# Modulation products over one k tile of 1024 columns instead of two of 512, with eight portions moved to earlier stages

## The reference

```python
c_act = jax.nn.silu(c)
cc_act = jax.nn.silu(c_ctx)
mod_x = jnp.split((c_act @ w_mod + b_mod)[:, None, :], 6, axis=-1)
mod_c = jnp.split(cc_act @ w_mod + b_mod, 6, axis=-1)
hx = modulate(rms_norm(x, g_pre_mix), mod_x[0], mod_x[1])
hc = modulate(rms_norm(xc, g_pre_mix), mod_c[0], mod_c[1])
...
y_x = jnp.concatenate([a_x, gla_out(gla_x, gx, out_g)], axis=-1) @ w_out
x = x + mod_x[2] * rms_norm(y_x, g_post_mix)
f_x = swiglu(modulate(rms_norm(x, g_pre_ffn), mod_x[3], mod_x[4]), w_ffn_in, w_ffn_out)
x = x + mod_x[5] * rms_norm(f_x, g_post_ffn)
```

## Time and profile before

| | before |
|---|---|
| median of 3 runs | 2784.82 us (2784.71 to 2785.11) |
| the profiled execution, span from first to last instruction | 2783.2 us |
| around the span (median less span) | 1.6 us |
| TensorE busy | 2765.4 us (99%) |
| VectorE busy | 2253.5 us (81%), 3613 instructions |
| ScalarE / GpSimd busy | 377.3 / 368.5 us |
| moved by DMA | 571.81 MB, 205 GB/s |

### The profile page before, as it was taken

How to read it: one execution, slowest core, us unless ns; L and a number is a source line. 1 busy time by engine, 2 the same in 40 slices (tenths; PEclk the granted TensorE clock), 3 DMA queues, 4 the chain that set the end, 5 groups by cost and what they waited for, 6 DMA issues and landing times.

```text
span 2783.2 us, 35947 instructions
## 1 busy us (share of the span) xinstructions
PE 2765.4 (99%) x13588; PEld 2424.0 (87%) x13588; DVE 2253.5 (81%) x3613; ACT 377.3 (14%) x713; POOL 368.5 (13%) x462
## 2 busy tenths in 40 slices
PE   9999999999999999999999999999999999999998
PEld 8888888888888888888888888888888888888887
DVE  7988888999999999998886568978888888766554
ACT  3221112001111111110002121211200000000000
POOL 1111221011112121120111002201011111000000
PEclk9999999999999999999999999999999999999999
DMA  8787666677676666667786455557566776566553
GB/s 273 239 254 226 209 205 204 216 244 227 212 210 209 210 212 212 206 227 270 263 265 178 144 159 144 158 160 227 175 216 213 220 220 204 173 174 190 174 174 121
DMA packets 276381, 571.81 MB, mean 205 GB/s; under 512 B 25370, under 2 KB 26778, under 8 KB 275696
## 3 DMA queue, kind: packets, MB, share of 16 engines
q1 hardware_dynamic: 244528, 460.18, 53.6%
q0 software_dynamic: 31248, 109.01, 12.4%
q10 hardware_dynamic: 432, 0.34, 0.0%
HBM read 565.49 MB, written 3.93 MB: 205 GB/s over the span
## 4 chain that ended last, share of the span: by engine, by line
PE 81%; issue 15%; DVE 1%; DMA 1%; POOLq 0%; POOL 0%; DVEq 0%; SPq 0%; ACT 0%
PE PS L565 76%; PE PS L646 1%; PE PS L608 1%; PE PS L740 0%; PE PS L709 0%; PE PS L575 0%; DMA ring<-in_w_in 0%; DVE x_tok L1719 0%; DMA x_tok<-in_x 0%; PE PS L1004 0%; PE PS L905 0%; PE PS L987 0%; PE PS L625 0%; PE PS L828 0%; POOL mem L2323 0%
## 5 line engine op out<-in xcount | busy, mean ns | idle before, releaser
L565 PE MATMUL PS<-sums,mem 128*128 128x256 f32 x4056 | 1206.3, 379 | 0.0
L565 PE MATMUL PS<-ring,mem 128*128 128x256 f32 x3788 | 1071.0, 379 | 0.0
L565 PEld LDWEIGHTS PS<-sums,mem 128*128 128x128 f32 x4056 | 770.6, 190 | 104.8
L565 PE MATMUL PS<-ring,act_t 128*128 128x256 f32 x3076 | 832.8, 379 | 0.1
L565 PEld LDWEIGHTS PS<-ring,mem 128*128 128x128 f32 x3788 | 715.5, 190 | 97.7 <-issue 1.6
L565 PEld LDWEIGHTS PS<-ring,act_t 128*128 128x128 f32 x3076 | 578.6, 190 | 77.5 <-issue 1.6
L1093 DVE TENSOR_TENSOR sums<-ring 128x512 f32<-128x512 f32 x431 | 312.2, 724 | 272.6 <-PE PS L565 242.4
L1214 DVE SCALAR_TENSOR_TENSOR mem<-mem,small 128x512 f32<-128x512 f32 x480 | 358.5, 768 | 36.3 <-DMA mem<-in_w_mod 5.6
L1103 DVE TENSOR_TENSOR sums<-sums,ring 128x512 f32<-128x512 f32 x431 | 306.6, 711 | 33.6 <-issue 1.3
L1105 DVE TENSOR_TENSOR sums<-sums,ring 128x512 f32<-128x512 f32 x431 | 303.0, 703 | 33.1 <-issue 1.3
L565 PE MATMUL PS<-sums,act_t 128*128 128x256 f32 x1092 | 324.8, 379 | 0.0
(11 more groups left out here) (277 smaller groups left out, 1266.2 us busy)
## 6 DMA issues: line engine op xcount, KB each, us to landing
ring<-in_w_in SPq DMA_DIRECT2D x240, 512.0 KB, 3.8
mem<-in_w_mod POOLq DMA_DIRECT2D x192, 512.0 KB, 5.0
ring<-in_w_up SPq DMA_DIRECT2D x176, 512.0 KB, 3.9
ring<-in_w_ffn_in SPq DMA_DIRECT2D x176, 512.0 KB, 3.7
ring<-in_w_down SPq DMA_DIRECT2D x88, 512.0 KB, 4.4
ring<-in_w_ffn_out SPq DMA_DIRECT2D x88, 512.0 KB, 3.8
ring<-in_w_out SPq DMA_DIRECT2D x64, 512.0 KB, 4.1
ring<-in_w_branch_a SPq DMA_DIRECT2D x16, 512.0 KB, 3.7
```

Source lines behind the costliest of these rows:

```text
L565: mm = pe.matmul(product(g, j), of(j, 2 * (c if part is None else part) + q), weights(j, n, q), start=lead and j in OPENS, stop=tail, skip ...
```

## The change

One load is now one k tile x 1024 columns (4 KB for each partition, 512 KB as before), and a portion is one product over 1024 columns for each vector, not two over 512. A block has 1024 columns and 16 portions. `acc` has one buffer of 1024 columns for each vector. The reduce at a block's end goes over 1024 columns. The number of portions stays 192. `HALVES` gives every unit of the gate stage three portions (the even ones had two), and the branch projections twelve instead of eight; the eight of the second output projection are gone. GpSimd's counts follow.

```diff
-MOD_BLOCKS = ([(b, False) for b in (16, 17, 18, 19, 14, 15, 8, 9)] + [(b, True) for b in range(8)]
-              + [(b, False) for b in (10, 11, 12, 13, 20, 21, 22, 23)])
+MOD_BLOCKS = ([(b, False) for b in (8, 9, 7, 4)] + [(b, True) for b in range(4)]
+              + [(b, False) for b in (5, 6, 10, 11)])
...
-    for _j in range(1, 4 if _k % 2 else 3):
+    for _j in range(1, 4):
         HALVES[N0["gate"] + 4 * _k + _j] = 1
-for _k in range(1, 16, 2):
-    HALVES[N0["branch"] + _k] = 1
+for _k in range(16):
+    if _k % 4 != 2:
+        HALVES[N0["branch"] + _k] = 1
...
-for _k in range(4, 12):
-    HALVES[N0["wout2"] + _k] = 1
...
-        wm = cut(26880, 2, 2, CN)
-        acc = cut(28928, 2, CN)
+        wm = cut(26880, 2, 2 * CN)
+        acc = [cut(28928, 2 * CN), cut(25856, 2 * CN)]
...
-                    b, part = h // 8, h % 8
+                    b, part = h // 16, h % 16
                     blk, two = MOD_BLOCKS[b]
-                    vectors = ((0, 0), (1, 16)) if two else ((b % 2, 16),)
+                    vectors = ((0, 0), (1, 16)) if two else ((0, 16),)
                     ve.drain()
                     ve.wait_ge(wm_loaded[h % 2], 16 * (h // 2 + 1))
-                    for k in range(2):
-                        if k:
-                            ve.drain()
-                        for which, at_ in vectors:
-                            col = c_vec[:, at_ + 2 * part + k:at_ + 2 * part + k + 1]
-                            if part + k == 0:
-                                op = ve.tensor_scalar(acc[:, which, :], wm[:, h % 2, k, :], col, None, MUL)
-                            else:
-                                op = ve.scalar_tensor_tensor(acc[:, which, :], wm[:, h % 2, k, :], col,
-                                                             acc[:, which, :], MUL, ADD)
+                    for which, at_ in vectors:
+                        col = c_vec[:, at_ + part:at_ + part + 1]
+                        if part == 0:
+                            op = ve.tensor_scalar(acc[which], wm[:, h % 2, :], col, None, MUL)
+                        else:
+                            op = ve.scalar_tensor_tensor(acc[which], wm[:, h % 2, :], col, acc[which], MUL, ADD)
                     op.then_inc(s["wm_used"], 1)
-                    if part == 7:
+                    if part == 15:
...
-                    kt, col = 2 * (h % 8), CN * MOD_BLOCKS[h // 8][0]
-                    pool.dma_start(wm[:, h % 2], w_mod[:, kt:kt + 2, col:col + CN]).then_inc(wm_loaded[h % 2], 16)
+                    kt, col = h % 16, 2 * CN * MOD_BLOCKS[h // 16][0]
+                    pool.dma_start(wm[:, h % 2], w_mod[:, kt, col:col + 2 * CN]).then_inc(wm_loaded[h % 2], 16)
...
-                mod_loads(2 + u % 2)
+                mod_loads(3)
...
-            mod_loads(22)
+            mod_loads(26)
...
-            mod_loads(7)
             post_rstd(0)
             ffn2_rstd()
-            mod_loads(1)
```

More of the change, by code:

```diff
@@ L87 @@
         HALVES[N0["up2"] + 8 * _k + _j] = 1
-assert sum(HALVES.values()) == 8 * len(MOD_BLOCKS)
-SUMS = [(0, 8, 16, N0["down"] + 25), (8, 20, 18, N0["down"] + 35), (20, 28, 20, N0["wout2"] + 13),
-        (28, 32, 24, N0["up2"] + 66)]
+assert sum(HALVES.values()) == 16 * len(MOD_BLOCKS)
+SUMS = [(0, 8, 8, N0["down"] + 25), (8, 20, 9, N0["down"] + 35), (20, 28, 10, N0["wout2"] + 13),
+        (28, 32, 12, N0["up2"] + 66)]
 SUMS_AFTER = {_n: _b for _b, (_, _, _, _n) in enumerate(SUMS)}
 for _, _, _blocks, _n in SUMS:
-    assert sum(HALVES.get(_k, 0) for _k in range(_n - 1)) >= 8 * _blocks
+    assert sum(HALVES.get(_k, 0) for _k in range(_n - 1)) >= 16 * _blocks
 BANK7, THROUGH7 = [], []
@@ L1200, in mod_halves @@
                     taken_halves[0] += 1
-                    b, part = h // 8, h % 8
+                    b, part = h // 16, h % 16
                     blk, two = MOD_BLOCKS[b]
-                    vectors = ((0, 0), (1, 16)) if two else ((b % 2, 16),)
+                    vectors = ((0, 0), (1, 16)) if two else ((0, 16),)
                     ve.drain()
                     ve.wait_ge(wm_loaded[h % 2], 16 * (h // 2 + 1))
-                    for k in range(2):
-                        if k:
-                            ve.drain()
-                        for which, at_ in vectors:
-                            col = c_vec[:, at_ + 2 * part + k:at_ + 2 * part + k + 1]
-                            if part + k == 0:
-                                op = ve.tensor_scalar(acc[:, which, :], wm[:, h % 2, k, :], col, None, MUL)
-                            else:
-                                op = ve.scalar_tensor_tensor(acc[:, which, :], wm[:, h % 2, k, :], col,
-                                                             acc[:, which, :], MUL, ADD)
+                    for which, at_ in vectors:
[4 more added lines that the diff above has]
+                            op = ve.scalar_tensor_tensor(acc[which], wm[:, h % 2, :], col, acc[which], MUL, ADD)
                     op.then_inc(s["wm_used"], 1)
-                    if part == 7:
+                    if part == 15:
                         ve.drain()
                         for which, at_ in vectors:
-                            to = mod_parts[:, (blk + at_ // 2) % 28]
-                            op = ve.tensor_reduce(to, acc[:, which].rearrange("p (b f) -> p b f", f=32), AX, ADD,
+                            first_ = (2 * blk + at_ // 2) % 28
+                            to = mod_parts[:, first_:first_ + 2, :].rearrange("p i c -> p (i c)")
+                            op = ve.tensor_reduce(to, acc[which].rearrange("p (b f) -> p b f", f=32), AX, ADD,
                                                   apply_transpose=True)
@@ L2412, in _ @@
             mod_loads(20)
-            pool.wait_ge(s["wm_used"], 152)
+            pool.wait_ge(s["wm_used"], 160)
             pool.dma_start(w_d[:], a["w_decay"]).then_inc(s["wd2_loaded"], 16)
@@ L2426, in _ @@
             pool.dma_start(tri[:], a["t_tri"]).then_inc(s["masks_loaded"], 16)
-            pool.wait_ge(s["job_acc"], 19)
+            pool.wait_ge(s["job_acc"], 10)
             pool.dma_start(level_mask[:], a["t_levels"]).then_inc(s["levels_loaded"], 16)
```

## The result

The changed kernel takes 2789.18 us, median of 20 runs (2787.60 to 2791.56), against 2784.93 us of the kernel before, median of 20 runs beside it (2784.28 to 2785.74). The ratio is 1.0016, 95% interval 1.0009 to 1.0022: 4.25 us slower, which is less than 0.2%. The forecast was 2788.0 us with a range of 2784.4 to 2791.6. The profiled execution has a span of 2787.5 us (2783.2 before); it is the run of 2789.35 us. One thing is new at once: the runs of the changed kernel spread over 4 us, those of the kernel before over 1.5 us. Of all the runs of this document one stands apart and is left out of its ratio: a run of the kernel with the branch's four portions elsewhere took 3375.07 us at a mean granted clock of 0.81, where the others have 1.00.

What follows compares the result with a forecast made beforehand. The prediction took TensorE as the bound, delayed only where VectorE is late: waits of 1.4 and 1.8 us, +3.2 us on the 2783.2 us span, plus the 1.6 us between span and median, gave 2788.0 us, range 2784.4 to 2791.6.

Steps and rivals of the forecast that it cites:

- What bounds the kernel: Whole kernel: TensorE works in 99% of the span, so the question is where VectorE is late, less what it saves.
- Prices of a portion: VectorE: a portion for one vector takes 1.37 us (0.29 less), one for two vectors 2.57 us (0.42 less).
- Branch projections: From 473.54 us VectorE gets ten portions, 13.7 us against 12.2 before, and ends branch_b(3) 1.5 us later.
- first wait: TensorE's new wait on VectorE after the branch projections, at the transposes that read branch_b(3): 1.4 us.
- First output projection: VectorE's work there grows from 31.0 to 35.2 us, 4.2 more, of which its existing waits absorb 1.93.
- second wait: TensorE's new wait on VectorE at the transposes that read wout_add(3), after the first up chunk: 1.8 us.
- Parts that cost nothing: Gate stage, up and down stages, second output projection: no cost; unit 2 keeps 0.4 us; VectorE about 56 us lighter.
- rival 4: Gate stage: unit 2's gather is late, up to 0.5 us, up to 2 us over all even units; chance 0.05.
- VectorE waiting inside the full stretch: Sign of a wrong forecast: VectorE waits between 473.5 and about 670 us, in the branch and first output projections.
- The width saves less: Branch and first output projections: wide portions cost 1.52 and 2.71 us, adding 6.8 us, 2791.6 us; chance 0.17.
- The stretch absorbs it: Branch and first output projections: products at 1.15 us and shrinking drained gaps give 2784.8 to 2786.2 us; chance 0.18.
- Relief counts: Emptier second output projection lets the norm chain behind it start earlier, faster, down to 2781.8 us; chance 0.05.

Runs made afterwards that it cites:

- ten drains: The changed kernel with ten drains that do nothing added ahead of VectorE's first wait: 2787.29 us, ratio 1.0010 to the kernel before.
- ones in the wait: The changed kernel with eight products of ones on TensorE just before its wait at turn_merged(3,0): 2788.07 us, ratio 1.0012 to the kernel before.
- the gate's four alone: The changed kernel with the branch's four extra portions moved to the down projection and the gate's four kept: 2784.60 us, ratio 0.9998 to the kernel before.
- narrow portions: The changed kernel's placement of portions, each made as before with two products of 512 columns: 2802.06 us, ratio 1.0060 to the kernel before.

## Why the prediction was right, and where it was off

The forecast was 3.2 us, measured were 4.25, inside the range. Step by step:

- **What bounds the kernel** held. TensorE's waits, not VectorE's total, decide: with the same 53 us less on VectorE the time is 2789.2 or 2784.4 us by where eight portions stand.
- **Prices of a portion** held: 1.38 us for 1.37. The product takes 1284 ns against 751 for half the width. The Trainium skill, "VectorE: DVE Perf Modes", section on the TRN2 errata, gives an fp32 addition (N+151)/0.96 ns, of which 157 ns are fixed; by that alone a portion would take an estimated 1.50 us. The trace has 1.38; that a drained gap goes with the instruction would be the rest.
- **Branch projections: mis-sized.** The term was +1.5 us and a first wait of 1.4. From the end of the last anchoring wait (473.54 us before, 472.87 after) to the end of `branch_b(3)` (566.36 before, 567.97 after) it is 2.3 us more. The ten portions were right; the rest is the two pauses, 0.86 us. With ten drains they are gone, the stretch is 1.5 us longer than before, as forecast, and the wait is 1.3 us. The step that failed is "It gets ten: 10 x 1.37 = 13.7 us" taken as the whole of what VectorE does there: it priced the instructions and not the pauses, whose place depends on the number of instructions ahead.
- **The clock** had no term. It stood at 1.00 after every wait between products in the profile before, the longest 1.3 us; after 2.1 us it did not. So the pauses cost twice in the profiled execution: 0.8 us of waiting and 1.7 us of slow products behind it.
- **First output projection: a little too high.** From `branch_b(3)` to the end of `wout_add(3)` it takes 99.90 us before and 103.38 after, 3.5 us more, and 4.2 - 1.93 + 0.38 + 0.91 = 3.6. The forecast had only the first two terms. That they agree so well is in part luck: with no wait of VectorE in the stretch it takes 101.69 us (ten drains) and 101.71 (ones in the wait), 1.8 us more than before, where 4.2 - 1.93 = 2.3 were forecast. So the work itself is 3.7 us more, not 4.2; which of its terms is too high was not measured. The second wait was forecast at 1.8 us and is 1.2, as the first had taken more of the same lateness and the slow products had delayed TensorE itself.
- **Parts that cost nothing** held: the run with the gate's four alone takes 2784.6 us, no wait of TensorE showed at unit 2 (rival 4) in the change, nor a new one after the second output projection. The margin there is as thin as forecast: with narrow portions TensorE lost some 0.9 us at unit 2, and with ten drains, where a pause of 0.46 us (at 321.5 us) falls into that gather, 0.2 us. The relief of VectorE was 53 us for "about 56", and the terms that the prediction lists for it add up to 59. GpSimd's issue became cheaper, 542 ns for 724.
- **Signs and rivals.** Of the signs named for a wrong forecast one did show, VectorE waiting inside the full stretch (0.38 and 0.91 us). Both waits follow the slow products and are gone where the clock stayed up. *The width saves less* falls with the portion's 1.38 us. *The stretch absorbs it* falls with the two waits. *Relief counts* falls, beyond 0.1%, with 2784.4 us where all relief and no lateness is left. The Trainium skill's rule on the same page, to minimize the op count on VectorE, is not contradicted by this: it speaks of VectorE's time, which did fall, but nobody waited for it.

Taken together: the lateness by portions alone costs 2.7 us (the run with ten drains, 2787.29 against 2784.60), and the pauses with the clock behind them the remaining 1.6 in the medians. The forecast of 3.2 us is 0.5 us above the first part, as its sum for `wout` was too high by that much, and 1 us below the whole, because two mechanisms were missing. That it came so near is in part luck, these errors standing against each other.

## What to carry to other kernels

Where one engine serves another for 100 us without slack, the lateness is the sum of prices from the last wait that anchors it; count the moved portions by what they become in their new place (twelve double ones for four), not by how many are moved. A change there has three parts: the work, the small pauses whose place depends on the number of instructions ahead of them, and what the waiting engine's clock does after the wait. Where such a wait can't be avoided, idle products in it can keep the clock up: here they cost no time that showed (0.2 us of waiting was left behind them).

## What the runs showed of the hardware

- **VectorE pauses some 0.4 us at every 128th instruction of its program** (395 to 483 ns from the end of one record, drains included, to the start of the next, in the 183 boundaries that showed), unless what falls there, a drain, a wait or a chunk's first sum, was queued behind a running instruction. Drains at the start moved the pauses out of the full stretch (ten), to four forecast places in it (eleven), and into it in the kernel before (eight at the forecast places, five not). What the engine does in them was not measured. Two kernels that differ by one idle instruction can differ by 2.7 us of 2790.
- **TensorE's granted clock fell to 0.50 behind waits of 1.96, 2.03, 2.05, 2.06, 3.2 and 4.8 us** and stood there for 3.4 us, with the longest wait 6.8 us, and stayed at 1.00 behind waits of 0.5 to 1.33 us and behind one of 1.89 us, in the profiled executions. The slow stretch behind a wait of 2 us cost TensorE 1.7 us. After 1.95 us of products of ones in place of the wait it stayed at 1.00.
- GpSimd issues a load of 128 rows of 4 KB in 542 ns and one of 256 rows of 2 KB in 724 ns; the queue's packets stay 31248 and the load's size is 512 KB in both.
